# Eight modulation chunks of the second layer move from TensorE products to VectorE sums, with a third buffer for them

## The reference, cut to what matters

```python
h = x * (1.0 + scale) + shift                    # _modulate, before the sublayer and before the experts
x = layer_norm(ALPHA * x + gate * sublayer(h))
# shift, scale, gate (six rows of 1024 a layer) = silu(c or c_ctx) @ mod_w[l] + mod_b[l]
```

## Time and profile before

| | |
|---|---|
| median of 3 runs (lowest to highest) | 1290.81 us (1288.6 to 1292.31) |
| the profiled execution | 1289.75 us, its span 1287.9 us |
| TensorE busy, share of the span | 1188.9 us, 92% |
| VectorE busy | 597.9 us, 46% |
| ScalarE busy | 352.0 us, 27% |
| mean granted TensorE clock | 0.978 |

### The profile page before, as it was taken

The page is one execution under the profiler, slowest core; times in us unless marked ns, Lnnn a source line. Parts: engine busy times, 40 slices in busy tenths (PEclk is TensorE's granted clock), DMA queues, the critical chain, the costliest instruction groups (busy, mean ns, idle before and its releaser), DMA issues.

```text
span 1287.9 us, 17510 instructions
## 1 busy us (share of the span) xinstructions
PE 1188.9 (92%) x6755; PEld 680.1 (53%) x6755; DVE 597.9 (46%) x1173; ACT 352.0 (27%) x695; POOL 186.9 (15%) x177
## 2 busy tenths in 40 slices
PE   5999999999999989999999877999999998999774
PEld 2554555545546577456555435755555555555441
DVE  2223333310136666768432217079986865332218
ACT  1333444421214543212122125311023111221122
POOL 1000000010000001131323120800000332222210
PEclk9999999999999999998999898999999998999988
DMA  9504476773211204826799969021114438999973
GB/s 348 210 25 177 142 254 239 289 270 114 89 33 40 74 10 163 340 83 232 299 407 409 406 244 393 23 91 66 66 66 171 156 128 316 392 410 408 354 293 150
DMA packets 99666, 269.79 MB, mean 209 GB/s; under 512 B 12811, under 2 KB 15154, under 8 KB 98690
## 3 DMA queue, kind: packets, MB, share of 16 engines
q1 hardware_dynamic: 83632, 234.55, 48.3%
q0 software_dynamic: 15632, 34.02, 7.1%
q10 hardware_dynamic: 322, 0.12, 0.0%
HBM read 257.68 MB, written 31.93 MB: 225 GB/s over the span
## 4 chain that ended last, share of the span: by engine, by line
PE 78%; DVE 6%; DMA 6%; SPq 4%; ACT 3%; issue 2%; ACTq 0%; POOLq 0%; DVEq 0%
PE ps L2285 18%; PE ps L2296 14%; PE ps L2797 8%; PE ps L2814 4%; PE ps L2175 4%; PE ps L2437 3%; DMA ln_rows<-in_moe_w_up 3%; PE ps L2600 3%; PE ps L2785 2%; PE ps L2581 2%; PE ps L2404 2%; PE ps L2746 2%; SPq L710 1%; PE ps L2699 1%; SPq L707 1%
## 5 line engine op out<-in xcount | busy, mean ns | idle before, releaser
L2285 PE MATMUL ps<-h_cm,weights 128*128 128x512 f32 (+1 forms) x832 | 226.8, 434 | 0.0
L2285 PEld LDWEIGHTS ps<-h_cm,weights 128*128 128x128 f32 x832 | 126.3, 191 | 104.0 <-issue 103.7
L2296 PE MATMUL ps<-weights,mix_cm 128*128 128x512 f32 x256 | 112.2, 595 | 0.0
L1769 DVE SCALAR_TENSOR_TENSOR scratch<-scratch,taps_cm 128x655 f32<-128x655 f32 x120 | 101.5, 897 | 2.5 <-ACT scratch L1325 1.0
L2296 PEld LDWEIGHTS ps<-weights,mix_cm 128*128 128x128 f32 x256 | 47.9, 190 | 56.5 <-issue 56.4
L2067 DVE TENSOR_TENSOR scratch<-ps,scratch 128x128 f32<-128x128 f32 x38 | 11.1, 292 | 143.1 <-ACT scratch L1373 143.1
L2296 PE MATMUL ps<-weights,h_cm 128*128 128x512 f32 (+1 forms) x208 | 71.4, 502 | 0.0
L2797 PE MATMUL ps<-weights,scratch 128*64 128x256 f32 x384 | 68.3, 389 | 1.8 <-DMA weights<-in_moe_w_up 1.8
L1442 DVE COPY mod_parts<-ps 128x512 f32<-128x512 f32 x24 | 16.6, 691 | 93.3 <-PE ps L2175 93.3
L1697 DVE SCALAR_TENSOR_TENSOR mix_cm<-mix_cm,gate_rows,ps 128x128 f32<-128x128 f32 x152 | 46.0, 345 | 25.1 <-PE ps L2545 23.0
L2296 PEld LDWEIGHTS ps<-weights,h_cm 128*128 128x128 f32 x208 | 36.3, 190 | 35.6 <-issue 35.6
(11 more groups left out here) (449 smaller groups left out, 2133.1 us busy)
## 6 DMA issues: line engine op xcount, KB each, us to landing
weights<-in_mod_w SPq DMA_DIRECT2D x13, 2048.0 KB, 8.9
x_tm<-in_mod_w SPq DMA_DIRECT2D x10, 2048.0 KB, 8.6
weights<-in_moe_w_gate SPq DMA_DIRECT2D x24, 512.0 KB, 11.6
weights<-in_moe_w_up SPq DMA_DIRECT2D x24, 512.0 KB, 13.4
weights<-in_moe_w_down SPq DMA_DIRECT2D x24, 512.0 KB, 15.7
scratch<-in_moe_w_down SPq DMA_DIRECT2D x21, 512.0 KB, 12.9
weights<-in_ab_w_in SPq DMA_DIRECT2D x5, 2048.0 KB, 12.8
weights<-in_cd_w_in SPq DMA_DIRECT2D x5, 2048.0 KB, 16.0
```

Of the source, the lines that this page charges most:

```text
L1769: ins = V.scalar_tensor_tensor(out=CO[:, j, 0:655], in0=UP[:, j, k:k + 655], scalar=CW[:, 4 * k + j:4 * k + j + 1], in1=CO[:, j, 0:655], o ...
L2285: ins = T.matmul(ps(*name)[:, a:b], w[:, k, col:col + 128], HT[:, k, a:b], start=(k == 0), stop=(k == KD - 1))
L2296: ins = T.matmul(ps(*name)[:, at:at + w.shape[2]], src[:, k, t * 128:t * 128 + 128], w[:, k, :], start=(k == 0), stop=(k == KD - 1))
```

## The change

Of the 24 chunks, the eight row chunks of layer 1, (1, 4) to (1, 11), are no longer multiplied on TensorE. `vec_mod` on VectorE multiplies each of the eight blocks of a chunk by its channel's value and adds it to an accumulator of 512 columns, once for each of the two conditioning vectors: 16 operations a chunk, each waiting for the one before. What is left to sum, the 128 partitions, is done by `vec_mod_sum` on TensorE with four matmuls of 256 columns against ones. `vec_mod_row` copies the result (half as wide as before), `store_vec_row` writes it in two transfers, and `mod_sums(1)` has only the bias to add. In attention 12 products are left in place of 16, in other steps than before; the turnings of (1, 0) to (1, 3), which were in steps 11, 12, 13 and 15, are in 13, 15, 16 and 18. The first vector chunk is begun in attention, three operations a step from step 16 (`VEC_STEPS`), the others follow under the projections. A sixth slot (5) lies in `scratch`, where keys and queries of attention were.

```diff
-ATTN_MODS = [(0, c) for c in range(4, 12)] + [(1, c) for c in range(8)]
-MOD_STEP = {5 * p + t: 4 * p + i for p in range(4) for i, t in enumerate((0, 1, 2, 4)) if p or t}
+ATTN_MODS = [(0, c) for c in range(4, 12)] + [(1, c) for c in range(4)]
+MOD_STEP = {n: i + 1 for i, n in enumerate((1, 2, 4, 5, 7, 9, 10, 12, 14, 15, 17))}
 KEY_STEP = {0: 1, 6: 2, 11: 3}
 QUERY_STEP = {3: 1, 8: 2, 13: 3}
-PROJ_MODS = {(0, 0): (1, 8), (0, 1): (1, 9), (0, 3): (1, 10), (1, 2): (1, 11)}
+VEC_MODS = list(range(4, 12))
+VEC_SUM_AT = {("hq", 0, 1): 4, ("hq", 0, 2): 5, ("hq", 0, 3): 6, ("hq", 1, 0): 7, ("hq", 1, 1): 8, ("hq", 1, 3): 9,
+              ("hv", 0): 10, ("hv", 2): 11}
+VEC_STEPS = {n: range(3 * (n - 16), 3 * (n - 16) + 3) for n in range(16, 20)}
...
                         g.append(("o", 3, 4))
-                    if (c, j) in PROJ_MODS:
-                        g.append(("mod",) + PROJ_MODS[c, j])
-            g += [("hv", t) for t in range(NT)]
+                    if ("hq", c, j) in VEC_SUM_AT:
+                        g.append(("modv", VEC_SUM_AT["hq", c, j]))
+            for t in range(NT):
+                g.append(("hv", t))
+                if ("hv", t) in VEC_SUM_AT:
+                    g.append(("modv", VEC_SUM_AT["hv", t]))
             g += [("slot", 0), ("y", 0, 0), ("slot", 2), ("oaT", 0), ("oaT", 2), ("slot", 1)]
...
         def slot3(s):
-            return W[:, 4096 * s:4096 * (s + 1)] if s < 3 else (OTF[:, 0:4096] if s == 3 else XF[:, 0:4096])
+            if s < 3:
+                return W[:, 4096 * s:4096 * (s + 1)]
+            return (OTF[:, 0:4096], XF[:, 0:4096], Z[:, 10240:14336])[s - 3]
         items = []
-        in_slot = [None, None, None, None, ("rows",)]
+        in_slot = [None, None, None, None, ("rows",), ("keys",)]
         words_in = [0, 0, 0, 0, 0]
         WITEM["rows",] = {"last": ("xT", 0, NT - 1)}
+        WITEM["keys",] = {"last": ("s", 7, 4)}
-            words_in[s] += 16 * len(parts)
-            WITEM[name] = {"slot": s, "full": s, "value": words_in[s], "parts": parts, "last": last, "before": in_slot[s]}
+            full = s if s < 5 else 3
+            words_in[full] += 16 * len(parts)
+            WITEM[name] = {"slot": s, "full": full, "value": words_in[full], "parts": parts, "last": last, "before": in_slot[s]}
             in_slot[s] = name
...
             mod_item(l, c, 4 if a % 2 else 1)
-            if a == 11:
+            if a == 8:
                 hq_item(1, 2)
-            if a == 13:
+            if a == 10:
                 hq_item(0, 0)
-        mod_item(1, 8, 1)
-        mod_item(1, 9, 4)
-        mod_item(1, 10, 1)
-        proj_item(("hv",), 1, ("hv", 4), w_in, 1536, 2048)
-        mod_item(1, 11, 4)
+        for c, s in zip(VEC_MODS, (1, 4, 5, 1, 4, 5, 4, 5)):
+            if c == 10:
+                proj_item(("hv",), 1, ("hv", 4), w_in, 1536, 2048)
+            mod_item(1, c, s)
         proj_item(("hfb",), 0, ("fb", 3), w_in, 1024, 1536)
         N_ITEMS0 = len(items)
-        in_slot[:] = [None, None, None, None, None]
+        in_slot[:] = [None] * 6
         for n, c in enumerate(CD_ORDER):
         MOD_DMAS = 16 * 10
-        ROW_MODS = [m for m in ATTN_MODS + [(1, c) for c in range(8, 12)] if m[1] >= 4]
+        ROW_MODS = [m for m in ATTN_MODS if m[1] >= 4]
+        VEC_PARTS = [z(14336, 1024).rearrange("p (g n) -> p g n", g=2), OTF[:, 0:1024].rearrange("p (g n) -> p g n", g=2)]
...
-                filled(sp, *WITEM[name]["last"])
+                if name[0] == "mod" and name[1] == 1 and name[2] in VEC_MODS:
+                    sp.wait_ge(mod_summed, 2 + VEC_MODS.index(name[2]))
+                else:
+                    filled(sp, *WITEM[name]["last"])
...
+            def store_vec_row(c):
+
+                emptied(sp, "modv", c)
+                for g in range(2):
+                    sp.dma_start(PARTD[1, 0, c // 2 - 2, g, 512 * (c % 2):512 * (c % 2) + 512].rearrange("(h n) -> h n", h=2),
+                                 MR[64 * g:64 * g + 64:32, c % 2, 0:256]).then_inc(d_mr[c % 2], 16)
+
             def load_parts(l):
                 for i in range(2):
-                    sp.wait_ge(d_mr[i], 64 * (4 * l + 4))
+                    sp.wait_ge(d_mr[i], 256 + 128 * l)
                 at_least(sp, d_mod, MOD_DMAS * l)
-                sp.dma_start(MOD_PARTS[l], PARTD[l].rearrange("j i g (k c) -> (i g k) j c", k=8)).then_inc(d_mod, 16)
+                if l == 0:
+                    sp.dma_start(MOD_PARTS[l], PARTD[l].rearrange("j i g (k c) -> (i g k) j c", k=8)).then_inc(d_mod, 16)
+                else:
+                    sp.dma_start(MOD_PARTS[l][:, 0, :], PARTD[l, 0].rearrange("i g (k c) -> (i g k) c", k=8)).then_inc(d_mod, 16)
                 for i in range(4):
...
-                sp.wait_ge(mod_summed, l + 1)
+                sp.wait_ge(mod_summed, 1 + l * (len(VEC_MODS) + 1))
                 sp.dma_start(MODD[l].rearrange("i g (k c) -> (i g k) c", k=8), MOD_SUM).then_inc(d_mod, 16)
...
                     load_item(n)
-                    if items[n] == ("mod",) + ATTN_MODS[14]:
+                    if items[n] == ("mod",) + ATTN_MODS[10]:
                         load_parts(0)
-                    if items[n] == ("mod",) + ATTN_MODS[15]:
+                    if items[n] == ("mod", 1, 4):
                         store_mods(0)
+                    if items[n][0:2] == ("mod", 1) and items[n][2] >= 8:
+                        store_vec_row(items[n][2] - 4)
                     if items[n] == ("hfb",):
-                        store_row(1, 11)
+                        for c in range(8, 12):
+                            store_vec_row(c)
                         load_parts(1)
...
+            def vec_mod(c, steps_of_it=range(16)):
+
+                it = WITEM["mod", 1, c]
+                acc = VEC_PARTS[c % 2]
+                w = slot3(it["slot"])[:, 0:4096].rearrange("p (k n) -> p k n", k=8)
+                for i in steps_of_it:
+                    k, g = i // 2, i % 2
+                    if i == 0:
+                        dve.wait_ge(w_full[it["full"]], it["value"])
+                    if k == 0:
+                        chain(V.tensor_scalar(acc[:, g, :], w[:, 0, :], CT[:, 0, g:g + 1], None, ALU.mult))
+                    else:
+                        ins = V.scalar_tensor_tensor(out=acc[:, g, :], in0=w[:, k, :], scalar=CT[:, k, g:g + 1], in1=acc[:, g, :],
+                                                     op0=ALU.mult, op1=ALU.add)
+                        if i < 15:
+                            chain(ins)
+                        else:
+                            ins.then_inc(mod_summed, 1)
+
+            def vec_mod_row(c):
+
+                filled(dve, "modv", c)
+                if c < 6:
+                    filled(dve, "modb", 1, c - 2)
+                else:
+                    dve.wait_ge(d_mr[c % 2], 256 + 32 * ((c - 4) // 2))
+                release(V.tensor_copy(MR[:, c % 2, 0:256], ps("modv", c)[:, 0:256]), "modv", c)
+
             def mod_sums(l):
                 chain(V.tensor_tensor(MOD_SUM, P[:, 0, :], MOD_BIAS, ALU.add))
+                if l:
+                    V.tensor_scalar(MOD_SUM[32:48, :], MOD_SUM[32:48, :], 1.0, None, ALU.add).then_inc(mod_summed, 1)
+                    return
                 chain(V.tensor_scalar(MOD_SUM[32:48, :], MOD_SUM[32:48, :], 1.0, None, ALU.add))
...
                     mod_row(*ATTN_MODS[MOD_STEP[n - 1]])
-                if n == 18:
+                if n == 15:
                     mod_sums(0)
-            mod_row(*ATTN_MODS[15])
+                if n in VEC_STEPS:
+                    vec_mod(VEC_MODS[0], VEC_STEPS[n])
+            vec_mod(VEC_MODS[0], range(12, 16))
+            for c in VEC_MODS[1:]:
+                vec_mod(c)
+                vec_mod_row(c - 1)
...
-            for c in range(2):
-                for j in range(4):
-                    if (c, j) in PROJ_MODS:
-                        mod_row(*PROJ_MODS[c, j])
+            value_rows(0)
             dve.wait_ge(h_zero, 5)
             decay_arguments(0)
-            mod_sums(1)
-            value_rows(0)
+            value_rows(1)
             emptied(dve, "hq", 0, 3)
             carried_rows(0)
-            for t in range(1, NT):
-                value_rows(t)
+            value_rows(2)
+            vec_mod_row(VEC_MODS[-1])
+            value_rows(3)
+            mod_sums(1)
+            value_rows(4)
             for i in range(20):
...
+            def vec_mod_sum(c):
+
+                pe.wait_ge(mod_summed, 2 + VEC_MODS.index(c))
+                open_group(pe, "modv", c)
+                for g in range(2):
+                    for h in range(2):
+                        at = 32 * (2 * g + h)
+                        ins = T.matmul(ps("modv", c)[at:at + 32, 0:256], const("ones")[:, 0:32],
+                                       VEC_PARTS[c % 2][:, g, 256 * h:256 * h + 256], start=True, stop=True)
+                close_group(ins, "modv", c)
+
             def side(kind, l, c):
```

(6 more changed lines are left out.)

## The result

The changed kernel took 1298.15 us (median of 14 executions, 1293.83 to 1301.97), the kernel before 1290.85 on the same chip (14 executions, 1288.19 to 1295.22). The ratio is 1.0048, with a 95% interval of 1.0037 to 1.0060: the change costs 7.3 us. The profiled execution of the changed kernel took 1300.03 us (span 1298.2), that of before 1289.75 (span 1287.9), so the two traces lie 10.3 us apart, 3 more than the medians.

A forecast was written before the change was run, and what follows sets the result against it. TensorE is busy 92% of the span; the question was where others wait for VectorE. -2.9 us to the first projection, +1.7 clock, +2.2 scan start, +1.7 clock: +2.7 on 1290.81 gives 1293.5 us, range 1285.5 to 1299.

The forecast's parts named there:

- forecast A: Waits in attention step 16 and before the scan, some clock loss: 1293.5 us (1289 to 1297); chance 0.50.
- Steps 0 to 15: Attention: two products gone from TensorE (-3.8 us), two turnings moved behind step 15 (-2.0 us).
- Step 16: Attention: VectorE waits 5.6 us for a weight load, delaying step 17's maximum; +2.9 us at the first projection, without clock.
- The clock: Behind TensorE's 5 us stand in step 16: +1.7 us, range 0 to 3.4; the same again at the scan's start.
- The projections: TensorE sums 0.6 us; VectorE chunk 12.1 us, 12.55 with copy; last sum ready 93.9 us after projections start.
- The scan's start: `mod_sums(1)` waits 6.5 us for transfers, TensorE stands 5 us; first projection to scan +2.2 us, clock +1.7 more.
- Behind S: After the scan's start (383.10 us in the trace of before) both kernels run the same rows; nothing added.
- B: VectorE's waits cost nothing extra, chunk 10.7 us, scan starts with TensorE's own end: -4.0 us, 1286.8; chance 0.12.
- C: Step 16's load of chunk (1, 4) is in time or hidden; scan still waits: -3.6 us, 1287.2; chance 0.12.
- D: Waits cost more: chunk 12.6 us (+3.0), clock at its bound at both places (+3.4): +9.1 us, 1299.9; chance 0.15.
- E: Both waits but no loss by the clock: -0.7 us, 1290.1; chance 0.07.

The follow-up runs named there:

- e4: Changed kernel with 24 unread 128x128 products on TensorE filling the stop in step 16: 1292.21 us, ratio 1.0004 to the kernel before.
- e2: Changed kernel with `mod_sums(1)` issued inside the scan's loop instead of ahead of the last value rows: 1291.32 us, ratio 0.9992 to the kernel before.
- e5: Changed kernel with four unread 128x512 products on TensorE between the last projection and the scan's wait: 1290.31 us, ratio 0.9978 to the kernel before.
- e9: Changed kernel with seven unread 128x512 products ahead of the scan: 1299.0 us, ratio 1.0052 to the kernel before.
- e8: The changed kernel again, unedited, on a second chip: 1297.8 us, ratio 1.0040 to the kernel before.
- e6: Changed kernel with each VectorE modulation operation waiting for the one two before, not its neighbour: 1291.32 us, ratio 0.9998 to the kernel before.
- e1: Changed kernel with chunk (1, 4) begun one step later, in step 17, when its weights have landed: 1287.04 us, ratio 0.9956 to the kernel before.
- e10: Kernel before with seven unread 128x512 products between its last projection and the scan: 1295.62 us, ratio 1.0023 to the kernel before.

## Why the prediction was off by 4.7 us

It said 1293.5 (range 1285.5 to 1299), most likely within 0.3% (0.42), and the kernel took 1298.15, 0.6% above before, which had got 0.33. The mechanism of forecast A came about in every step that the text names; the sizes of the clock terms were too small, and one place was missing. That the time still lies in the range, 0.85 us under its edge, is owed in part to errors of the other sign, 0.6 us in item 1 and 1.9 in item 5.

1. *Steps 0 to 15.* -5.8 forecast, -6.4 measured.
2. *Step 16.* The wait of 5.60 us for the load, 8.0 us from issue to landing, and the maximum behind it came as worked out: 249.42, against 255.4 - 5.8 = 249.6. From the product of step 15 to H, +2.9 without the clock; measured +8.1 (9.0 - 0.9). By e4, 4.5 of them are the clock up to the product of step 17, and 3.3 at H; that leaves 3.6 to 4.8 for the stop.
3. *The clock.* This is the step whose size failed. I took +1.7 us with 3.4 as the upper bound, out of one gap of 1.11 us with 6.8 us at the lower level. The stop here was five times as long and so was not like that row: the clock stayed down for 13.6 us, and its share was 3.3 to 4.5 us, at my bound or above it. A bound taken from one short gap need not hold for a long one.
4. *The projections.* A sum of TensorE is 0.64 us (0.6 forecast), VectorE's beat from start to start 0.788 (0.787), a chunk with its copy 12.29 (12.55). The sum of chunk 11 was ready 92.4 us behind H in place of 93.9.
5. *The scan's start.* `mod_sums(1)` did wait for the transfers and TensorE for the last copy, but H to S grew by 0.3 us and not by 2.2, since VectorE was 1.5 us ahead. The wait itself was 3.26 us and not 5. The clock behind it cost 2.8 us by S to K, in place of 1.7 and inside its bound of 3.4; e2 and e5 take it away.
6. *Behind S* the text said that both kernels run the same rows, and so added nothing; that the clock could differ over the same rows it did not ask. The rows are the same, but behind K they took 5 us longer in the profile. e9 shows that the same work takes either time when it comes 2.7 us later, and that the half clock at the scan's start is not needed for it.

In sum, in the profiles: +0.5 start, -6.4, +8.1 from step 15 to H, +0.3, +2.8, +5.0 = +10.3. The medians are 7.3 apart, since this profile of the changed kernel lies 1.9 us above its median and that of before 1.1 below. The terms up to K make +4.8 of them (-6.4 + 8.1 + 0.3 + 2.8), 2.1 more than the forecast of +2.7. What is left for the part behind K is 2.5, and 0.8 by e8's median (1297.8 - 1292.16 - 4.8); these two are estimates, since no trace shows the other executions.

Of the rivals, B had its mechanism wrong for this kernel, since the wait for the neighbour costs time, as the two beats of the earlier trace rows said. Brought about by e6, it takes the scan's wait away as described, but 1291.3 and not 1286.8 comes out, since step 16 is dearer. C's condition is brought about by e1. Its time (1287.2) is that of e1 (1287.04) in part by luck: e1 is 5.6 us under the kernel before on its chip, where C said 3.6, the gain at H being larger (9.5 us against the changed kernel) and the scan's clock still falling. D named nearly the right time (1299.9) with half of the right cause: the chunk was not dearer (12.0 us and not 12.6), but the clock cost nearly its bound at both places (3.3 and 2.8 us for 3.4 each). E, no loss by the clock, was wrong at both places.

What stays open: why the falls behind K come in some runs and not in others that reach K at the same time (e2, e6), why e10 shows them in its profile and not in its median, and where the 4.7 us by which e5 gains more than the clock's 2.8 lie in the executions without a trace. That the kernel before's wait for a load ahead of the product of step 17 (1.04 us) is gone was read from the traces and not tested by itself.

## What to carry to other kernels

Before work is moved to an idle engine, find the operation behind which it lands in that engine's queue, and the earliest moment at which its data can be there: a chunk that began one step too soon, and one wait placed ahead of a copy, turned a gain of 12 us into a loss of 7. Price each new stop of TensorE twice, for its length and for the slower clock that follows, and take the second from a stop of like length; if the stop can't be removed, idle products that end with it give most of the second part back (e4, e5). Products that last longer than the stop can cost far more than their length (e9). When two kernels differ by a few us in a part that the edit doesn't touch, compare the granted clock there and delay the start of that part before looking for a cause in the edit; e10 shows that the answer can stay unclear.

## What was not expected of the hardware

- A small delay can move the falls of the clock in the rest of the program. 2.7 us of added products (e5 to e9) made the kernel 8.7 us slower, and 9.3 against the kernel before on each chip; 6.2 us of them in the kernel before (e10), of which 4.8 came through to S, made it only 4.0 slower.
- Much of the spread of one kernel goes with this clock. In the 29 executions of the kernel before on the chip of e1 to e4, the mean granted clock went from 0.970 to 0.980, and the span correlates with it by -0.81, with 8.9 us for each 0.01 (a correlation; nothing was varied). The changed kernel's median was 0.967 in 14 executions.
- Two VectorE operations that don't wait for one another overlap: with a duration of 0.744 us each they started 0.663 us apart in e6, where neighbours that wait started 0.788 apart with 0.752.
